# Three weight loads of a mixture-of-experts trunk moved from SyncE's queue to ScalarE's

## The reference

```
h2 = rms_norm(x, norm2_g[l])
# router: one of 4 groups, then 2 of its 8 experts, so 32 experts in all
for each expert e:
    gt, up = split(xb @ w_gate_up[l, e], 2)      # [rows, 1024] @ [1024, 1024]
    y = (silu(gt) * up) @ w_down[l, e]           # [rows, 512] @ [512, 1024]
x = x + sum over a token's two experts of weight * y
```

## Time and profile before

| | |
|---|---|
| Median of 3 runs | 1316.64 us |
| The profiled execution's own time | 1316.96 us |
| Its span | 1315.1 us |
| PE busy | 1124.5 us (86%) |
| DVE, ACT, POOL busy | 417.9, 199.6, 165.5 us |
| Mean granted PE clock | 0.934 |
| DMA, whole span | 462.72 MB, mean 352 GB/s |
| Chain that ended last | PE 66%, DMA 28% |
| Gate-up loads in that chain | 26% |

### The profile page before, as it was taken

The page is one execution under the profiler, slowest core; times in us unless marked ns, Lnnn a source line. Parts: engine busy times, 40 slices in busy tenths (PEclk is TensorE's granted clock), DMA queues, the critical chain, the costliest instruction groups (busy, mean ns, idle before and its releaser), DMA issues.

```text
span 1315.1 us, 17981 instructions
## 1 busy us (share of the span) xinstructions
PE 1124.5 (86%) x7434; PEld 509.5 (39%) x7435; DVE 417.9 (32%) x859; ACT 199.6 (15%) x439; POOL 165.5 (13%) x186
## 2 busy tenths in 40 slices
PE   9999999999766696569899999999996766775697
PEld 6445546433321232123264455464332312331232
DVE  5799733311100111011185996232111101110111
ACT  4423404000000000000054224030000000000000
POOL 1767300000000000000044762000000000000000
PEclk9999999999978897789999999999998878987899
DMA  8533687999999999999974326979999999999997
GB/s 275 184 129 129 256 343 298 383 426 428 434 428 426 431 435 428 425 430 424 404 219 170 126 88 256 391 275 424 423 428 433 431 431 426 435 431 428 425 421 302
DMA packets 61985, 462.72 MB, mean 352 GB/s; under 512 B 20488, under 2 KB 20704, under 8 KB 40416
## 3 DMA queue, kind: packets, MB, share of 16 engines
q1 hardware_dynamic: 60880, 461.70, 85.0%
q10 hardware_dynamic: 1040, 0.09, 0.1%
HBM read 460.73 MB, written 1.05 MB: 351 GB/s over the span
## 4 chain that ended last, share of the span: by engine, by line
PE 66%; DMA 28%; SPq 3%; issue 1%; DVE 1%; ACT 1%; DVEq 0%
DMA pool_all<-in_w_gate_up_dram 26%; PE ps L1135 23%; PE ps L857 9%; PE ps L1151 4%; PE ps L891 4%; PE ps L731 4%; PE ps L916 3%; PE ps L1050 2%; PE ps L1082 2%; PE ps L710 2%; PE ps L741 2%; PE ps L872 2%; DMA pool_all<-in_w_down_dram 2%; SPq L538 2%; SPq L634 2%; PE ps L775 1%
## 5 line engine op out<-in xcount | busy, mean ns | idle before, releaser
L1135 PE MATMUL ps<-pool_all,xs 128*32 128x512 f32 (+1 forms) x2816 | 332.5, 631 | 158.6 <-DMA pool_all<-in_w_gate_up_dram 157.0
L1135 PEld LDWEIGHTS ps<-pool_all,xs 128*32 128x32 f32 x2816 | 91.7, 116 | 391.9 <-issue 389.7
L1151 PE MATMUL ps<-pool_all,early 128*32 128x512 f32 (+1 forms) x1408 | 160.3, 605 | 23.0 <-ACT early L1487 13.4
L1941 DVE SCALAR_TENSOR_TENSOR rope<-rope,ps 128x512 f32<-128x512 f32 x22 | 15.1, 687 | 505.7 <-ACT rope L1485 505.7
L857 PE MATMUL ps<-pool_all,hT 128*128 128x512 f32 x256 | 114.6, 598 | 0.0
L1485 ACT ACTIVATE rope<-ps 128x512 f32<-128x512 f32 x22 | 13.1, 597 | 626.6 <-PE ps L1135 626.6
L1151 PEld LDWEIGHTS ps<-pool_all,early 128*32 128x32 f32 x1408 | 44.9, 111 | 123.9 <-issue 121.2
L2230 POOL TENSOR_TENSOR pool_all<-pool_all 128x512 f32<-128x512 f32 x64 | 79.8, 1278 | 37.3 <-DVE pool_all L1717 37.3
L1082 PE MATMUL ps<-xs,cst 128*128 128x512 f32 x176 | 81.4, 605 | 0.0
L1050 PEld LDWEIGHTS ps<-cst,hT 128*128 128x128 f32 x640 | 73.0, 192 | 16.8 <-issue 16.8
L1050 PE MATMUL ps<-cst,hT 128*128 128x128 f32 x640 | 76.8, 278 | 0.0
(11 more groups left out here) (262 smaller groups left out, 1020.0 us busy)
## 6 DMA issues: line engine op xcount, KB each, us to landing
pool_all<-in_w_gate_up_dram SPq DMA_DIRECT2D x38, 4096.0 KB, 27.7
pool_all<-in_w_down_dram SPq DMA_DIRECT2D x58, 2048.0 KB, 21.8
pool_all<-in_w_gate_up_dram SPq DMA_DIRECT2D x34, 2048.0 KB, 15.6
pool_all<-in_w_in_dram SPq DMA_DIRECT2D x12, 2048.0 KB, 11.4
pool_all<-in_w_gate_up_dram SPq DMA_DIRECT2D x24, 1024.0 KB, 11.8
pool_all<-in_w_gate_up_dram SPq DMA_DIRECT2D x24, 512.0 KB, 12.7
pool_all<-in_w_glu_dram SPq DMA_DIRECT2D x4, 2048.0 KB, 10.8
pool_all<-in_w_out_dram SPq DMA_DIRECT2D x4, 2048.0 KB, 12.1
```

The source lines that it names most:

```text
L1135: mm = pe.matmul(ps[r, half], xT[:, k // 4, k % 4, r], lane_cols(n, h, k % 4, half), start=(k == 0), stop=(k == KC - 1), skip_group_check= ...
L1151: mm = pe.matmul(ps[r, 2 + half], ffT[:, c, r], lane_cols(n, 2, c, half), start=(c == 0), stop=(c == 3), skip_group_check=True)
```

## The change

SP no longer issues the home loads of units 4, 6 and 8. ACT issues them, on its own DMA queue, from its loop over units: after all three of its activations of unit 2j it issues the home load of unit 2j+2, and goes on to unit 2j+1. The loop now has three turns of two units. Sizes, addresses, slots and the semaphore counted by PE are the same. ACT's instruction order stands in for a semaphore wait: it can't have copied unit 2j's down half before that unit's gate-up, which read slots 9 and 10, was done.

```
             for u in range(4, BRANCH):
-                load_home(u, 0 if u % 2 else 9)
+                if u % 2:
+                    load_home(u, 0)
                 load_rest(u)
-            load_home(BRANCH, 9)
...
-            with act.Fori(2, BRANCH) as i:
-                main_unit(i)
+            with act.Fori(1, BRANCH // 2) as j:
+                main_unit(j * 2)
+                act.dma_start(pair_rows(9), flat(wgu_d[bass.ds(j * (2 * TRIO) + (l * EXPERTS + TRIO), 1)])).then_inc(landed[9], 16)
+                main_unit(j * 2 + 1)
```

## The result

The changed kernel takes 1335.32 us, the median of 4 runs (1334.58 to 1336.34), against 1316.60 before (one run more than the median of 1316.64 above): a ratio of 1.0142, 95% interval 1.0129 to 1.0154. That is 18.7 us more; the prediction said 19.2 more, 1335.8. The span went from 1315.1 to 1333.6.

What follows compares the result with a forecast made beforehand. The experts' stage was taken as bound by DMA bytes, so only idle DMA time costs: 2 gaps x 2 layers x 4.8 = +19.2 us on 1316.6, other terms 0, giving 1335.8 us; range 1326 to 1344.

Steps and rivals of the forecast that it cites:

- What bounds the stage: Experts' stage of each layer: bound by bytes; only the rate and time with idle DMA engines can change its length.
- SP's and ACT's issues at 0: Six SP issues of 0.43 us saved and six ACT issues of 0.44 us added, both hidden by waiting: 0.
- The pairs 9.8 us late: Unit 5's pairs share the DMA engines equally with ACT's home load and land at 426.9 instead of 417.1.
- Rival B: ACT's queue gets a small share: 1328.6 us at a third, 1318 at a quarter; chance 0.10.
- rival A: Order of issue decides across the queues, pairs land at 417.1 as before: no change, 1316.6 us; chance 0.07.
- The gap: Under gate-ups 5 and 7 the queue runs dry before SP's next pairs: 4.8 us each, 3.3 to 6.3.
- Where: Gaps fall in gate-ups 5 and 7 of each layer; gate-up 3 has a backlog, even units keep their filler: 0.
- Absorbed later?: After the gaps: no, as DMA share is 1.01 until 653.26 and the last unit's pieces move with gate-up 9.
- Rate: While both queues have work, some 118 us, the rate could differ by -1.9 to +4.2 us; taken as 0.
- D's disturbance: Two queues disturb each other, 415 GB/s for 118 us, and gate-ups 1.5 us longer: 1346.0 us; chance 0.06.
- C's gain: With two queues open the rate goes to 437 GB/s: -1.9 us, 1314.8 us; chance 0.03.

Runs made afterwards that it cites:

- unit 4 alone: Against the kernel before, only unit 4's home load is issued by ACT, those of units 6 and 8 by SP; 1316.93 us against 1316.94.
- SP behind the pairs: Against the kernel before, SP issues home loads of units 6 and 8 directly behind the pairs of units 5 and 7, ahead of the downs; 1316.82 us against 1316.94.
- ACT in mid gate-up: Changed kernel, but ACT waits until part 0 of the following odd unit's gate-up is done before issuing the home load; 1316.92 us, 0.9999 of the kernel before.
- padded before: Kernel before plus idle matmuls between part 0 and part 1 of gate-ups 3, 5 and 7; 1317.00 us against 1317.00.
- the one with more gaps: Changed kernel, with ACT also issuing the home loads of units 5 and 7; 1350.05 us against 1316.95 for the kernel before.
- unit 6's load alone: Against the kernel before, only unit 6's home load is issued by ACT, the others by SP; 1325.47 us, ratio 1.0062.
- ACT issues late: Changed kernel, but ACT waits for the even unit's last down matmul before issuing the home load; 1334.97 us against 1317.00 for the kernel before.

## Why the prediction was right

**What bounds the stage.** Right: it is bytes plus holes. Every kernel without a hole is within 0.2 us of the kernel before, whatever the order, the queue and PE's extra work (four kernels: unit 4 alone, SP behind the pairs, ACT in mid gate-up, padded before). Every kernel with holes is slower. For the changed kernel (below) and the one with more gaps, the lengthened periods add up to the loss to within 0.5 us.

**SP's and ACT's issues at 0.** ACT's issues took 0.34 to 0.37 us beside its idle time; ACT in mid gate-up shows their price is nothing.

**The pairs 9.8 us late.** Measured 9.5 (426.57 against 417.10). I had taken equal shares and left the share of ACT's queue open above 0.38. The queue table shows 4.19 MB of 8.00 while both were served, 0.52, so the equal shares were right. Rival B needed less than 0.38, rival A no sharing; both are out for this kernel, B by the share and A by the lateness of the pairs. One part was off without harm: I had the home load's first bytes 1.5 us after its issue. It was issued at 397.91, and from 397.9 to 401.4 the queue table lists no bytes of q10, so it was 3.5 us. That is why it landed 23.4 us after its issue and not about 20; it was still in before the pairs.

The Trainium skill's page "DMA: Bandwidth & Descriptors", section "Queues, rings and completion order", has the DMA engines take turns between the rings packet by packet. The trace agrees: 0.52 for the home load, where even turns would give 0.50. The same page's "Issuing engines are not separate DMA queues" says that a second issuing engine saves only issue time. The runs agree that it gains nothing, and add that it can cost 18.7 us or nothing, by its moment.

**The gap.** From gate-up 5 to 6 it was 38.46, predicted 38.9. Two terms were off, and in opposite directions. SP's issue came 442.87 - 426.57 = 16.3 us after the start of gate-up 5, where I had 17.0, because gate-up took 16.2 and not 16.9. From the issue to gate-up 6 it took 465.03 - 442.87 = 22.2 us, where I had 19.5 + 2.4 = 21.9. I had taken the longer gate-up because of the longer idle; that reason was wrong, as the last section shows.

The other three gaps, with the kernel before's period from gate-up 7 to 8 as the last row. That period is 45.44 us even there, since it has more bytes (427 GB/s over it are 19.4 MB):

```profile
518.62:558.77 40.15, 31.36 (x239) 12.01 (x239) 4.89 (x8) 1.77 (x3) 0.00 (x0) 0.88 0.91 381
1087.56:1127.59 40.03, 31.90 (x238) 12.09 (x239) 4.80 (x8) 1.77 (x3) 0.00 (x0) 0.88 0.88 369
1181.19:1220.71 39.52, 31.16 (x238) 11.93 (x239) 4.89 (x8) 1.77 (x3) 0.00 (x0) 0.89 0.89 373
```

```profile
504.85:550.29 45.44, 31.02 (x238) 11.95 (x239) 4.88 (x8) 1.77 (x3) 0.00 (x0) 0.84 1.00 427
```

Without a hole these would be 34.1 us behind a gate-up 5 and 45.4 - 9.8 = 35.7 behind a gate-up 7. So the gaps are 4.3 and 4.5 in layer 0, 5.9 and 3.9 in layer 1. The sum is 18.6, the mean 4.6; the prediction had 4.8 each. The 5.9 is partly a gate-up of 16.8 us, and partly a load that took 23.1 us from issue (1104.46) to gate-up 6, 0.9 more than in layer 0, which is not explained. The kernel with unit 6's load alone has the like: 5.1 us for its one gap in layer 1 (1083.99 to 1123.15), of which 1.3 come back from gate-up 7 to 8 (44.16 us in place of 45.45). So part of the 5.9 may belong to the 3.9. Single gaps miss the predicted 4.8 by up to 1.1 us, so that the total is only 0.5 us off is in part luck.

**Where.** Gate-up 3 at 0, gate-ups 5 and 7 with a gap: shown by moving single loads. The stall in gate-up 3 was foreseen as 8.5 us from 330.4 to 338.9 and was 8.51, ending at 338.72.

**Absorbed later?** No. Gate-up 9 is 8.3 us late in layer 0, gate-up 4 of layer 1 still 8.3 and its gate-up 9 18.5, and the span is 18.5 longer.

**Rate.** I took 0. While both queues were busy (all but the ends of 401 to 421 us) it was 436 GB/s, within 1.5% of the 430 of the steady periods:

```profile
401.00:421.00 20.00, 3.75 (x12) 1.44 (x8) 1.45 (x3) 0.00 (x0) 0.00 (x0) 0.66 1.01 436
```

So D's disturbance isn't there, and C's gain, if it is one, is 0.3 us per load. One queue alone had 437 over a like stretch, so nothing here speaks for a gain.

No version beat the kernel before. In the steady units none of this kind is likely to: its queue has no hole there (share 1.00), and a different order moves no byte.

## What to carry to other kernels

Where transfers bound a stage, ask of each load not when it arrives but what it covers: the queue must have enough work for the whole of each stretch in which its issuer waits for compute, plus the 2.4 us that an issue to an empty queue has on top of its transfer. A load with slack is best left where it bridges such a stretch. Sending it early on another queue takes turns away from loads with no slack now and leaves the first queue dry later; if it must go on another queue, tie its issue to the start of the compute it is to bridge.

## What the runs showed of the hardware

Two queues with large loads shared the DMA engines with no loss of rate (436 GB/s together) and nearly evenly: 4.19 of 8.00 MB for the queue with one 4 MB load beside the queue with two. A load that was issued while the engines were busy with the other queue's loads had its first bytes 3.5 us later (397.91 to 401.4). On the empty queue it was 0.9 to 1.1 us (442.87, SP's issue, to between 443.8 and 444.0). What makes up the rest of the 2.4 us of the earlier trace rows isn't shown.

The granted clock when gate-up 5 began was 0.50 (1.2 GHz) in both kernels, after 11 us of idle PE and after 21.8. In the kernel before it rose in the window from 420 to 421 us, some 3 us after the start; in the changed kernel in the one from 431 to 432, some 4.5 us after it. So gate-up had about 1.5 us more at half of 2.4 GHz, worth about 0.75 us (an estimate), and it took 16.18 us against 15.40. The changed kernel first, then the kernel before:

```profile
427.00:430.00 3.00, 3.00 (x19) 0.64 (x15) 0.00 (x0) 0.00 (x0) 0.00 (x0) 0.50 0.98 415
430.00:431.00 1.00, 1.00 (x12) 0.35 (x8) 0.00 (x0) 0.00 (x0) 0.00 (x0) 0.50 1.12 475
431.00:432.00 1.00, 1.00 (x16) 0.28 (x12) 0.00 (x0) 0.00 (x0) 0.00 (x0) 0.94 0.96 410
```

```profile
418.00:420.00 2.00, 2.00 (x16) 0.56 (x12) 0.00 (x0) 0.00 (x0) 0.00 (x0) 0.50 0.98 418
420.00:421.00 1.00, 1.00 (x12) 0.25 (x8) 0.00 (x0) 0.00 (x0) 0.00 (x0) 0.95 1.12 475
```

The length of the idle time doesn't set this. The kernel in which ACT issues late has a gate-up 5 of 15.24 us after 21.09 us of idle PE in layer 1, and the earlier trace rows one of 16.88 after 11.17. What sets the moment of the rise isn't shown.

```profile
1088.02 15.24 PE L1135 MATMUL ps<-pool_all,xs 128*32 x128 [21.09 <-DMA pool_all<-in_w_gate_up_dram]
```
